# Decoder trunk on one core: the row of r by way of device memory instead of by turns on TensorE

## The chip, the cores and the metric

The kernel runs on one core of a Trainium2 chip. The metric is the device time of one execution in microseconds (us). Each kernel is run several times and the median is given.

## The reference

Two layers (DEPTH 2) of a decoder over 256 tokens (SEQ) with a width of 1024 (D). Every layer has four sub-layers, each with an RMS norm ahead of it and one behind it:

```
f = swiglu(rms_norm(h, ffn1_pre_g), ffn1_w_gu, ffn1_w_down);  h = h + 0.5 * rms_norm(f, ffn1_post_g)
u = rms_norm(h, mix_pre_g);  sb_q, sb_k, sb_v, df_q, df_k, df_v, g_sb, g_df = split(u @ w_in)
    # stick-breaking attention on sb_*, differential attention with rotary on df_*, gates, w_out
f = swiglu(rms_norm(h, ffn2_pre_g), ffn2_w_gu, ffn2_w_down);  h = h + 0.5 * rms_norm(f, ffn2_post_g)
    # then a gated per-layer embedding (w_ple_gate, w_ple_proj)

swiglu(x, w_gu, w_down) = (silu(g) * u) @ w_down,  g, u = split(x @ w_gu)        # d_ff = 2816
rms_norm(x, g) = x * r * g,  r = 1 / sqrt(mean(x * x) + eps), one number for each token
```

The inner norm's r is one number for each of the 256 tokens. It can be multiplied in behind the matrix product, since the product is linear.

## The kernel before

**Where things lie.** Tokens in natural layout: 128 tokens on the partitions, in two tiles t = 0, 1. `r_pre` is [128, 2]: the scale of token 128t + p stands on partition p, column t. A product in natural layout takes it as a scalar for each partition. In a "flat" product the outputs stand with the features on the partitions and the 256 tokens along the row. Then r is needed as a row of 256 numbers that is the same on all 128 partitions: that is `r_cols`, 256 columns of the tile `prob`.

**Who does what.** Weights come in units of 1 MB into `raw` (three slots, issued from SyncE). ScalarE (ACT) rounds a unit into `w_hi`, times the norm's gain (`high`). VectorE (DVE) writes the rest into `w_lo` (`low`). TensorE (PE) multiplies with three products for each exact one. GpSimd (POOL) computes r: `rsqrt_mean`, by `pre_norm` for the inner norms and `post_norm` for the outer ones. Its DMA queue is used at the start only, for gains and positions. Each engine has one fixed order of instructions, written out by hand; semaphores tie them together.

**An FFN** runs over 11 blocks (NC) of 256 hidden features, c = 0 to 10. Each takes three units: gate and up in two halves, then down. Block 0 and block 10 are natural; blocks 1 to 9 are flat. In a flat block VectorE's `flat_gate` adds the two halves of g (L1152), multiplies by r_cols (L1154), waits for ScalarE's silu (L726), multiplies by r_cols again (L1156), adds the two halves of u (L1158) and takes the product (L1161). Behind it stands the `low` of the second half of the next block (L1106), which TensorE needs in the middle of that block's gate and up.

**How r_cols is made before.** VectorE's `spread_r` copies r_pre over 256 columns of `mixed_t` (L1144). TensorE's `turn_r` transposes these in two turns into PSUM (L1625). ScalarE's `keep_r` copies them to r_cols (L720). This happens six times: in each layer for stage 0 (first FFN), stage 1 (mixer, for the stick-breaking q and k, used in `add_flat`, L1331) and stage 2 (second FFN). In an FFN turn_r stands in the middle of block 1, just ahead of `turn_first_ht` (L1632); in the mixer it stands behind unit m = 2.

Of the kernel before, what the change touches and what calls it, by code (L numbers as in the profile page):

```python
# [77 lines left out]
def trunk_kernel(nc, a, out):  # L78
    with ExitStack() as ctx:
# [9 lines left out]
        def bank(b):  # L89
            return ps[:, b, :]  # L90
# [2 lines left out]
            return ps[:, b:b + 2, :].rearrange("p b n -> p (b n)")  # L93


        raw = sb("raw", [P, SLOTS, UNIT])
        w_hi = sb("w_hi", [P, SLOTS, UNIT], F32R)
        w_lo = sb("w_lo", [P, SLOTS, UNIT], F32R)
# [74 lines left out]

        x_hi, x_lo = x_both[:, 0, :, :], x_both[:, 1, :, :]
        glu_g, glu_u = glu[:, 0, :, :], glu[:, 1, :, :]
        r_spread = mixed_t[:, 0:SEQ].rearrange("p (t n) -> p t n", t=TT)
        r_cols = prob[:, 0:1, 0:SEQ]
        e_ple = gates[:, 1, :, :]
        p_nat = soft[:, :, 0:PLE]
# [22 lines left out]
        g_scaled = sem("g_scaled")  # L202
        silu_scaled = sem("silu_scaled")
        h_done = sem("h_done")
        r_wide = sem("r_wide")
        r_turned = sem("r_turned")
        r_kept = sem("r_kept")
        ht_turned = sem("ht_turned")
        ht_high = sem("ht_high")
# [97 lines left out]
        HT_BANK, P_BANK, FIRST_P_BANK = 6, 7, (3, 5)  # L307
        GU_BANK = (4, 5)
        FLAT_BANK = (6, 7, 4, 5)
        FIRST_HT_BANK, R_BANK = 2, 3  # L310
        flat_g, flat_u = ([ps[:, b:b + 2, n * SEQ:(n + 1) * SEQ] for n in range(2)] for b in FLAT_BANK[::2])
        WIN_BANK = ((4, 5), (2, 3))
        DOWN_PAIR = (0, 2)
# [178 lines left out]
        def _(pool):  # L492
# [67 lines left out]
            def post_norm(i, n, order):  # L560
                for t in range(TT):
                    pool.wait_ge(squared_post, post_count(i, n, t))
                    rsqrt_mean(i, order + t, mean_post[:, t:t + 1], ms_post[:, t:t + 1], r_post[:, t:t + 1],
                               eps_half if FACTOR[n] == 0.5 else eps_norm).then_inc(post_scale, 1)

            def close(i):

                for t in range(TT):
                    pool.wait_ge(squared_post, post_count(i, 3, t))
                    rsqrt_mean(i, 18 + t, mean_post[:, t:t + 1], ms_post[:, t:t + 1], r_post[:, t:t + 1],  # L570
                               eps_norm).then_inc(post_scale, 1)
# [15 lines left out]

            for i in range(DEPTH):
                pre_norm(i, 0, 0)
                if i == 0:  # L590
                    pool.wait_ge(sines, 1)
                    pool.tensor_scalar(rope_s[:, :, 0:32], rope_s[:, :, 32:64], -1.0, None, ALU.mult
                                       ).then_inc(rope_ready, 1)
                    pool.tensor_copy(rope_c[:, :, 32:64], rope_c[:, :, 0:32]).then_inc(rope_ready, 1)
                post_norm(i, 0, 2)
                pre_norm(i, 1, 4)

                pool.wait_ge(pre_scale, 8 * i + 4)
                pool.tensor_tensor(r_query[:, :], r_pre[:, :], q_factor[:, :], ALU.mult).then_inc(query_scale, 1)
                for hd in range(DF_HEADS):  # L600
                    pool.wait_ge(d_eps, 4 * i + hd + 1)
                    pool.wait_ge(d_square, 4 * i + hd + 1)
                    rsqrt_mean(i, 6 + hd, mean_sub[:, :], ms_sub[:, :], r_sub[:, :], sub_eps
                               ).then_inc(d_scale, 1)
                post_norm(i, 1, 10)
                pre_norm(i, 2, 12)
                post_norm(i, 2, 14)
                pre_norm(i, 3, 16)
                if i < LAST:
                    close(i)  # L610
                else:
                    close_last(i)
# [3 lines left out]
        def _(act):  # L616
# [98 lines left out]
                act.wait_ge(h_done, FLAT * (2 * i + f) + c)  # L715
                act.activation(ht_hi[:, :, :], glu_u, ACT.Copy).then_inc(ht_high, 1)

            def keep_r(i, stage, b=R_BANK):
                act.wait_ge(r_turned, nth_r(i, stage))
                act.activation(r_cols[:, 0, :], bank(b)[:, 0:SEQ], ACT.Copy).then_inc(r_kept, 1)  # L720

            def flat_glu(i, f, c, u0):
                act.wait_ge(gu_done, 2 * NC * i + NC * f + c + 1)
                act.activation(glu_g, flat_g[1], ACT.Copy).then_inc(low_kept, 1)
# [21 lines left out]
            def ffn(i, f, u0, g0, next_unit, loads):  # L746

                if f:
                    first_silu(i, f, u0)
                high(i, u0 + 3, g0 + 4, halves=(0,))  # L750
                act.wait_ge(pre_scale, 8 * i + 4 * f + 2)
                silu(i, f, 0, u0 + 1, 1)
                high(i, u0 + 3, g0 + 4, halves=(1,))
                high(i, u0 + 4)
                keep_r(i, 2 * f)
                high_first_ht(i, f)
                high(i, u0 + 5, g0)
                flat_glu(i, f, 1, u0)
                high(i, u0 + 6, g0 + 4)
                with act.Fori(2, NC - 1) as c:  # L760
                    high(i, u0 + 1, c=c)
                    high_ht(i, f, c - 1)
                    high(i, u0 + 2, g0, c=c)
                    flat_glu(i, f, c, u0)
                    high(i, u0 + 3, g0 + 4, c=c)
                loads()
                high(i, u0 + 3 * NC - 2)
                high_ht(i, f, NC - 2)
                high(i, u0 + 3 * NC - 1)
                silu(i, f, NC - 1, u0 + 3 * NC - 3, 0)  # L770
                act.wait_ge(ht_split, 2 * HTS * i + HTS * f + NC - 1)
                silu(i, f, NC - 1, u0 + 3 * NC - 3, 1)
                high_last_ht(i, f, 0)
                next_unit()
                high_last_ht(i, f, 1)
# [65 lines left out]
            def mixer(i):  # L841
                for m in range(23):
# [28 lines left out]
                        diff_exp(i, DF_SCORE[m])  # L871
                    if m in DF_TURN:
                        diff_square(i, DF_TURN[m])
                    if m == 2:
                        keep_r(i, 1, QK_PAIR)
                    if m in (4, 6):
                        k = (m - 4) // 2
                        act.wait_ge(qk_turned, 2 * i + k + 1)
# [160 lines left out]
        def _(dve):  # L1039
# [98 lines left out]
                dve.tensor_tensor(ht_lo[:, :, :], src, ht_hi[:, :, :].bitcast(F32), ALU.subtract  # L1138
                                  ).then_inc(ht_split, 1)

            def spread_r(i, first=False):
                if first:
                    dve.wait_ge(const_all, 1)
                dve.tensor_copy(r_spread, r_pre[:, :].rearrange("p (t o) -> p t o", o=1).to_broadcast([P, TT, P])  # L1144
                                ).then_inc(r_wide, 1)

            def flat_gate(i, f, c):
                n = FLAT * (2 * i + f)
                wide_r = r_cols.to_broadcast([P, 2, SEQ])
# [25 lines left out]
            def ffn(i, f, u0, g0, next_unit):  # L1175
                if (i, f) not in BESIDE_INPUTS:
                    product(i, f, 0, 0)
                low(i, u0 + 3, g0 + 4, halves=(0,))
                product(i, f, 0, 1)
                spread_r(i, (i, f) == (0, 0))  # L1180
                low(i, u0 + 3, g0 + 4, halves=(1,))
                low(i, u0 + 4)
                low_ht(i, f, 0, bank(FIRST_HT_BANK).rearrange("p (k n) -> p k n", k=2))
                low(i, u0 + 5, g0)
                dve.wait_ge(r_kept, nth_r(i, 2 * f))
                flat_gate(i, f, 1)
                low(i, u0 + 6, g0 + 4)
                with dve.Fori(2, NC - 1) as c:
                    low(i, u0 + 1, c=c)
                    low_ht(i, f, c - 1, glu_u)  # L1190
                    low(i, u0 + 2, g0, c=c)
                    flat_gate(i, f, c)
                    low(i, u0 + 3, g0 + 4, c=c)
                if (i, f) == (0, 0):
                    fold_cosine()
                low(i, u0 + 3 * NC - 2)
                low_ht(i, f, NC - 2, glu_u)
                low(i, u0 + 3 * NC - 1)
                for t in range(TT):
                    product(i, f, NC - 1, t)  # L1200
                low_last_ht(i, f, 0)
                next_unit()
                low_last_ht(i, f, 1)
# [117 lines left out]
            def add_flat(i, j, x):  # L1321

                n = 4 * i + 2 * (j - SBQ) + x + 1
                dst = (sbq_t, sbk_t)[j - SBQ][:, 2 * x:2 * x + 2, :]
                dve.wait_ge(flat_kept, n)
                dve.scalar_tensor_tensor(out=dst, in0=flat_pair(SB_FLAT[j][x])[0],
                                         scalar=SB_D ** -0.5 if j == SBQ else 1.0, in1=flat_copy,
                                         op0=ALU.mult, op1=ALU.add).then_inc(flat_added, 1)
                dve.wait_ge(flat_added, n)
                dve.wait_ge(r_kept, nth_r(i, 1))  # L1330
                dve.tensor_tensor(dst, dst, r_cols.to_broadcast([P, 2, SEQ]), ALU.mult).then_inc(sb_ready, 1)  # L1331

            def mixer(i):
                if i == 0:
                    dve.wait_ge(rope_ready, 2)
                dve.wait_ge(pre_scale, 8 * i + 4)
                spread_r(i)
                dve.wait_ge(query_scale, i + 1)
                for m in range(23):

# [200 lines left out]
        def _(pe):  # L1541
# [77 lines left out]
                        elif s == 1 and done is not None:  # L1619
                            mm.then_inc(done, 1)  # L1620

            def turn_r(i, stage, b):
                pe.wait_ge(r_wide, nth_r(i, stage))
                for t in range(TT):
                    mm = pe.transpose(bank(b)[:, t * P:(t + 1) * P], r_spread[:, t, :], ident[:, :])  # L1625
                mm.then_inc(r_turned, 1)

            def turn_first_ht(i, f):
                turn_r(i, 2 * f, R_BANK)
                for k in range(2):  # L1630
                    for t in range(TT):
                        mm = pe.transpose(bank(FIRST_HT_BANK)[:, k * SEQ + t * P:k * SEQ + (t + 1) * P],  # L1632
# [23 lines left out]
            def ffn(i, f, q, u0, before_last):  # L1656
# [58 lines left out]
                def step(c, at, first=False):  # L1715
# [6 lines left out]
                    if first:  # L1722
                        turn_first_ht(i, f)
                    flat_gate_up(u0, 1, c, at)
                    if first:
                        pe.wait_ge(r_kept, nth_r(i, 2 * f))
                    down(u0 + 1, c - 1, first=first, c=at)

                def first_gate_up(s, t, before):
# [134 lines left out]

            def behind(i, m):

                if m == 2:
                    turn_r(i, 1, QK_PAIR)
                if m == 4:
                    pe.wait_ge(r_kept, nth_r(i, 1))  # L1870
                    pe.wait_ge(roped, 4 * i + 2)
                    turn_four(pair(QK_PAIR), df_slabs[0]).then_inc(qk_turned, 1)
                if m == 6:
# [241 lines left out]
```

## Time and profile before

| | |
|---|---|
| median of 3 runs | 1174.3 us (1174.22 to 1174.74) |
| the profiled execution | 1173.8 us; its span from the first to the last instruction 1172.1 us |
| granted TensorE clock, mean over the span | 0.999 of full speed |
| TensorE busy | 1163.3 us, 99% of the span |
| VectorE, ScalarE, GpSimd busy | 850.1, 720.6 and 51.6 us (73%, 61%, 4%) |
| DMA from memory | 213.68 MB read, 183 GB/s over the span |

The times in the trace are microseconds from the first instruction. A line such as L1625 is the line of the kernel that issues the instruction. PEld is TensorE's load of the stationary tile, which overlaps the multiplication before it. So the distance from one load's start to the next is what an instruction costs TensorE in a dense stretch. A row of the timeline merges equal instructions: start, time in all, engine, line, operation, tiles, shape, count.

### The profile page before, as it was taken

To read this page: it belongs to the slowest core of one execution; us is meant where nothing else is said; L and a number is where in the kernel's file an instruction comes from. 1 tells how busy PE (TensorE), PEld (TensorE's weight loads), DVE (VectorE), ACT (ScalarE), POOL (GpSimd) and SP (SyncE) were. 2 spreads that over 40 slices of the span, in tenths; PEclk is the share of its full clock that TensorE was granted. 3 is DMA by queue.
4 is the path that set the end of the run, shared out by engine and by line. 5 is a ranking of instruction groups with operands and counts; after the bars stand their busy time and mean duration, and the time that the engine had idled before them with its cause. 6 is when DMAs were issued, how large, how long until landed. Compare 5 with 4: busy or idle time off the path is not lost.

```text
span 1172.1 us, 17196 instructions
## 1 busy us (share of the span) xinstructions
PE 1163.3 (99%) x6031; PEld 983.4 (84%) x6031; DVE 850.1 (73%) x1290; ACT 720.6 (61%) x1166; POOL 51.6 (4%) x124
## 2 busy tenths in 40 slices
PE   9999999999999999999999999999999999999997
PEld 7888888888888888888888888888888888888886
DVE  6766777977857776676787776678776677677666
ACT  7555556677765655555685655565776566565555
POOL 4000001000000000000100000010000010000002
PEclk9999999999999999999999999999999999999999
DMA  9656565654354555655556565756534456656551
GB/s 296 217 189 205 176 216 164 220 179 145 128 196 144 194 201 189 205 176 210 180 173 200 173 207 180 243 172 192 169 109 179 164 162 214 194 172 207 182 194 37
DMA packets 138655, 215.37 MB, mean 184 GB/s; under 512 B 6958, under 2 KB 97904, under 8 KB 138608
## 3 DMA queue, kind: packets, MB, share of 16 engines
q1 hardware_dynamic: 135808, 208.43, 53.4%
q10 hardware_dynamic: 2576, 6.29, 1.6%
q8 instruction: 28, 0.46, 0.2%
q14 instruction: 19, 0.16, 0.0%
q0 software_dynamic: 224, 0.04, 0.0%
HBM read 213.68 MB, written 1.05 MB: 183 GB/s over the span
## 4 chain that ended last, share of the span: by engine, by line
PE 99%; DVE 0%; issue 0%; POOL 0%; ACT 0%; POOLq 0%; DVEq 0%
PE ps L1671 23%; PE ps L1544 19%; PE ps L1546 18%; PE ps L1545 18%; PE ps L1681 12%; PE ps L1914 3%; PE ps L1591 2%; PE ps L1923 1%; PE ps L1800 1%; PE ps L1815 1%; PE ps L1774 0%; PE ps L1786 0%; PE ps L2006 0%; PE ps L1829 0%; PE ps L1836 0%
## 5 line engine op out<-in xcount | busy, mean ns | idle before, releaser
L1106 DVE SCALAR_TENSOR_TENSOR w_lo<-raw,g_layer,w_hi 128x512 fp32r<-128x512 f32 (+1 forms) x504 | 356.3, 767 | 139.1 <-ACT w_hi L644 139.1
L644 ACT ACTIVATE w_hi<-raw,g_layer 128x512 fp32r<-128x512 f32 (+1 forms) x524 | 346.7, 732 | 113.7 <-PE ps L1681 97.0
L1671 PE MATMUL ps<-x_both,w_hi 128*128 128x512 f32 x1152 | 287.7, 392 | 0.0
L1671 PEld LDWEIGHTS ps<-x_both,w_hi 128*128 128x128 f32 x1152 | 209.3, 189 | 39.4 <-issue 0.4
L1544 PE MATMUL ps<-w_hi,x_both 128*128 128x512 f32 x576 | 231.6, 402 | 0.0
L1546 PE MATMUL ps<-w_hi,x_both 128*128 128x512 f32 x576 | 224.9, 390 | 0.0
L1545 PE MATMUL ps<-w_lo,x_both 128*128 128x512 f32 x576 | 224.5, 390 | 0.0
L1103 DVE TENSOR_TENSOR w_lo<-raw,w_hi 128x1024 fp32r<-128x1024 f32 x114 | 134.8, 1220 | 61.3 <-ACT w_hi L641 61.3
L641 ACT ACTIVATE w_hi<-raw 128x1024 fp32r<-128x1024 f32 x114 | 114.7, 1052 | 92.7 <-PE ps L1546 92.6
L1681 PEld LDWEIGHTS ps<-x_both,w_lo 128*128 128x128 f32 x1152 | 152.6, 191 | 8.4
L1681 PE MATMUL ps<-x_both,w_lo 128*128 128x256 f32 x1152 | 156.0, 283 | 0.0
L1544 PEld LDWEIGHTS ps<-w_hi,x_both 128*128 128x128 f32 x576 | 108.2, 188 | 25.8 <-issue 3.0
L1546 PEld LDWEIGHTS ps<-w_hi,x_both 128*128 128x128 f32 x576 | 108.1, 188 | 23.3
L1545 PEld LDWEIGHTS ps<-w_lo,x_both 128*128 128x128 f32 x576 | 108.4, 188 | 19.9
L1544 PE MATMUL ps<-w_hi,ht_hi 128*128 128x512 f32 x320 | 124.9, 390 | 0.0
L1546 PE MATMUL ps<-w_hi,ht_lo 128*128 128x512 f32 x320 | 124.6, 389 | 0.0
L1545 PE MATMUL ps<-w_lo,ht_hi 128*128 128x512 f32 x320 | 124.5, 389 | 0.0
L726 ACT ACTIVATE glu<-glu 128x512 f32<-128x512 f32 x36 | 22.8, 633 | 78.5 <-DVE glu L1154 78.5
L1546 PEld LDWEIGHTS ps<-w_hi,ht_lo 128*128 128x128 f32 x320 | 60.1, 188 | 12.5
L1545 PEld LDWEIGHTS ps<-w_lo,ht_hi 128*128 128x128 f32 x320 | 60.1, 188 | 12.3
L1544 PEld LDWEIGHTS ps<-w_hi,ht_hi 128*128 128x128 f32 x320 | 60.1, 188 | 12.3
L1156 DVE TENSOR_TENSOR glu<-glu,prob 128x512 f32<-128x512 f32 x36 | 24.9, 693 | 27.6 <-ACT glu L726 27.6
(230 smaller groups left out, 1039.1 us busy)
## 6 DMA issues: line engine op xcount, KB each, us to landing
raw<-in_ffn_w_gu SPq DMA_DIRECT2D x170, 512.0 KB, 4.6
raw<-in_ffn_w_down SPq DMA_DIRECT2D x88, 512.0 KB, 4.0
raw<-in_w_in SPq DMA_DIRECT2D x80, 512.0 KB, 4.5
raw<-in_w_out SPq DMA_DIRECT2D x16, 512.0 KB, 4.0
raw<-in_w_ple_gate SPq DMA_DIRECT2D x16, 512.0 KB, 3.7
raw<-in_w_branch_sb SPq DMA_DIRECT2D x8, 512.0 KB, 4.1
raw<-in_w_branch_diff SPq DMA_DIRECT2D x8, 512.0 KB, 4.0
raw<-in_ffn_w_gu SPq DMA_DIRECT2D x12, 256.0 KB, 7.4
```

The source lines that it names most:

```text
L641: last = act.activation(w_hi[:, s, part], raw[:, s, part], ACT.Copy)
L644: last = act.activation(w_hi[:, s, part], raw[:, s, part], ACT.Copy, scale=g_layer[:, g:g + 1])
L1103: last = dve.tensor_tensor(w_lo[:, s, part], raw[:, s, part], whi[:, part], ALU.subtract)
L1106: last = dve.scalar_tensor_tensor(out=w_lo[:, s, part], in0=raw[:, s, part], scalar=g_layer[:, g:g + 1], in1=whi[:, part], op0=ALU.mult, o ...
L1156: dve.tensor_tensor(glu_g, glu_g, wide_r, ALU.mult).then_inc(silu_scaled, 1)
L1544: pe.matmul(dst, x_h, w_h, start=first, stop=False, **group)
L1545: pe.matmul(dst, x_h, w_l, start=False, stop=False, **group)
L1546: return pe.matmul(dst, x_l, w_h, start=False, stop=last, **group)
L1591: mm = pe.transpose(x_bank(i, q, idx)[:, k * P:(k + 1) * P], src[:, (4 * n + k) * P:(4 * n + k + 1) * P], ident[:, :])
L1671: mm = pe.matmul(dst, w_hi[:, s, cols], x_both[:, :, 4 * half + k, :], start=half == 0 and k == 0, stop=stop and k == 3, skip_group_check= ...
L1681: mm = pe.matmul(bank(FLAT_BANK[j])[:, 0:SEQ], w_lo[:, s, cols], x_hi[:, 4 * half + k, :], start=False, stop=False, skip_group_check=True)
L1914: mm = pe.matmul(dst, w_hi[:, s, cols], x_both[:, :, 4 * half + k, :], start=half == 0 and k == 0, stop=stop and k == 3, skip_group_check= ...
```

## The change

GpSimd makes the row by three DMAs and no other engine has a part in it. For each stage, behind both r's, it writes r_pre[:, 0] and r_pre[:, 1] (128 numbers of 4 bytes each, one for each partition) to a row of a buffer in device memory, waits until both are there, and reads the row of 256 numbers (1 KB) back to all 128 partitions of r_cols. spread_r, turn_r and keep_r go, and so do TensorE's two waits for r_kept. VectorE's waits for r_kept stay where they were and count by 16.

```
+            def keep_row(i, stage):
+
+                n = nth_r(i, stage)
+                for t in range(TT):
+                    pool.wait_ge(pre_scale, 8 * i + 2 * stage + t + 1)
+                    pool.dma_start(r_rows[n - 1, t * P:(t + 1) * P].rearrange("(p o) -> p o", o=1), r_pre[:, t:t + 1]
+                                   ).then_inc(r_written, 16)
+                pool.wait_ge(r_written, 32 * n)
+                pool.dma_start(r_cols[:, 0, :], r_rows[n - 1, :].partition_broadcast(P)).then_inc(r_kept, 16)
...
             for i in range(DEPTH):
                 pre_norm(i, 0, 0)
+                keep_row(i, 0)
...
                 pool.tensor_tensor(r_query[:, :], r_pre[:, :], q_factor[:, :], ALU.mult).then_inc(query_scale, 1)
+                keep_row(i, 1)
...
                 pre_norm(i, 2, 12)
+                keep_row(i, 2)
                 post_norm(i, 2, 14)
...
-            def keep_r(i, stage, b=R_BANK):
-                act.wait_ge(r_turned, nth_r(i, stage))
-                act.activation(r_cols[:, 0, :], bank(b)[:, 0:SEQ], ACT.Copy).then_inc(r_kept, 1)
...
-            def spread_r(i, first=False):
-                if first:
-                    dve.wait_ge(const_all, 1)
-                dve.tensor_copy(r_spread, r_pre[:, :].rearrange("p (t o) -> p t o", o=1).to_broadcast([P, TT, P])
-                                ).then_inc(r_wide, 1)
...
-                dve.wait_ge(r_kept, nth_r(i, 2 * f))
+                dve.wait_ge(r_kept, 16 * nth_r(i, 2 * f))
                 flat_gate(i, f, 1)
...
-                dve.wait_ge(r_kept, nth_r(i, 1))
+                dve.wait_ge(r_kept, 16 * nth_r(i, 1))
                 dve.tensor_tensor(dst, dst, r_cols.to_broadcast([P, 2, SEQ]), ALU.mult).then_inc(sb_ready, 1)
...
-            def turn_r(i, stage, b):
-                pe.wait_ge(r_wide, nth_r(i, stage))
-                for t in range(TT):
-                    mm = pe.transpose(bank(b)[:, t * P:(t + 1) * P], r_spread[:, t, :], ident[:, :])
-                mm.then_inc(r_turned, 1)
-
             def turn_first_ht(i, f):
-                turn_r(i, 2 * f, R_BANK)
...
                     flat_gate_up(u0, 1, c, at)
-                    if first:
-                        pe.wait_ge(r_kept, nth_r(i, 2 * f))
                     down(u0 + 1, c - 1, first=first, c=at)
...
-                if m == 2:
-                    turn_r(i, 1, QK_PAIR)
                 if m == 4:
-                    pe.wait_ge(r_kept, nth_r(i, 1))
                     pe.wait_ge(roped, 4 * i + 2)
```

## Rows read from the trace of the kernel before

**Rows 1.** The page: span and busy time of each engine.

```profile
span 1172.1 us, 17196 instructions
PE 1163.3 (99%) x6031; PEld 983.4 (84%) x6031; DVE 850.1 (73%) x1290; ACT 720.6 (61%) x1166; POOL 51.6 (4%) x124
```

**Rows 2.** Who PEld waited for: us in total, times, longest.

```profile
PEld ps L1544 <- DVE x_both L1133: 2.5, 10, 0.3
PEld ps L1591 <- DVE h L1222: 1.8, 9, 0.2
```

**Rows 3.** PEld timeline about turn_r: first FFN and mixer of layer 1.

```profile
610.02 0.24 PEld L1625 LDWEIGHTS ps<-ident,mixed_t 128*128 128x128 f32 x2
610.24 0.47 PEld L1632 LDWEIGHTS ps<-ident,glu 128*128 128x128 f32 x4
...
794.83 0.19 PEld L1546 LDWEIGHTS ps<-w_hi,x_both 128*128 128x128 f32 x1
795.06 0.37 PEld L1625 LDWEIGHTS ps<-ident,mixed_t 128*128 128x128 f32 x2
795.40 0.19 PEld L1544 LDWEIGHTS ps<-w_hi,x_both 128*128 128x128 f32 x1
795.51 0.19 PEld L1545 LDWEIGHTS ps<-w_lo,x_both 128*128 128x128 f32 x1
```

**Rows 4.** The tiles prob and mixed_t: durations ns min/median/max, first and last start.

```profile
L720 ACT ACTIVATE prob<-ps x6: 383/384/384, 31.1 to 974.8; 128x256 f32<-128x256 f32 x6
L1144 DVE COPY mixed_t<-r_pre x6: 280/281/317, 27.6 to 970.5; 128x256 f32<-128x256 f32 x6
```

**Rows 5.** POOL timeline: the last r of stages 0, 1 and 2 (layer 0), 0 (layer 1).

```profile
25.00 0.55 POOL L552 TENSOR_TENSOR r_pre<-ms_pre,neg_half 128x1 f32<-128x1 f32 x1
208.38 0.19 POOL L599 TENSOR_TENSOR r_query<-r_pre,q_factor 128x2 f32<-128x2 f32 x1
386.71 0.55 POOL L552 TENSOR_TENSOR r_pre<-ms_pre,neg_half 128x1 f32<-128x1 f32 x1
604.44 0.55 POOL L552 TENSOR_TENSOR r_pre<-ms_pre,neg_half 128x1 f32<-128x1 f32 x1
```

**Rows 6.** DVE timeline: first use of r_cols and what follows, by the same stages.

```profile
36.77 0.69 DVE L1154 TENSOR_TENSOR glu<-glu,prob 128x512 f32<-128x512 f32 x1
...
40.54 2.73 DVE L1106 SCALAR_TENSOR_TENSOR w_lo<-raw,g_layer,w_hi 128x512 fp32r<-128x512 f32 x4
232.53 0.69 DVE L1331 TENSOR_TENSOR sbq_t<-sbq_t,prob 128x512 f32<-128x512 f32 x1
401.05 0.69 DVE L1154 TENSOR_TENSOR glu<-glu,prob 128x512 f32<-128x512 f32 x1
404.51 2.73 DVE L1106 SCALAR_TENSOR_TENSOR w_lo<-raw,g_layer,w_hi 128x512 fp32r<-128x512 f32 x4
616.20 0.69 DVE L1154 TENSOR_TENSOR glu<-glu,prob 128x512 f32<-128x512 f32 x1
```

**Rows 7.** PE timeline: block 2 of the first FFN of layer 0.

```profile
46.98 2.08 PE L1681 MATMUL ps<-x_both,w_lo 128*128 128x256 f32 x16
```

**Rows 8.** pos_i's issues; the landings of pos_i, lam_layer, post_g, out_h, in this order.

```profile
L504 POOL DMA_DIRECT2D pos_i<-in_positions x2: 547/572/597, 4.5 to 5.1; - x2
DMA to landing us min/median/max: 5.6/5.6/5.6
...
DMA to landing us min/median/max: 4.5/5.4/6.3
...
DMA to landing us min/median/max: 3.3/5.1/7.1
...
DMA to landing us min/median/max: 2.0/2.0/2.1
```

**Rows 9.** One of POOL's and one of DVE's rows at the end of the second FFN.

```profile
568.85 1.26 POOL L550 TENSOR_TENSOR ms_pre<-mean_pre,eps_norm 128x1 f32<-128x1 f32 x1 [3.42 <-ACT tmp L682]
568.78 2.47 DVE L1106 SCALAR_TENSOR_TENSOR w_lo<-raw,g_layer,w_hi 128x1024 fp32r<-128x1024 f32 x2
```

More of the change, by code:

```diff
@@ L93, in pair @@
             return ps[:, b:b + 2, :].rearrange("p b n -> p (b n)")
+        r_rows = nc.dram_tensor("r_rows", (3 * DEPTH, SEQ), F32, kind="Internal").ap()
         raw = sb("raw", [P, SLOTS, UNIT])
@@ L175, in trunk_kernel @@
         glu_g, glu_u = glu[:, 0, :, :], glu[:, 1, :, :]
-        r_spread = mixed_t[:, 0:SEQ].rearrange("p (t n) -> p t n", t=TT)
         r_cols = prob[:, 0:1, 0:SEQ]
@@ L204, in trunk_kernel @@
         h_done = sem("h_done")
-        r_wide = sem("r_wide")
-        r_turned = sem("r_turned")
+        r_written = sem("r_written")
         r_kept = sem("r_kept")
@@ L309, in trunk_kernel @@
         FLAT_BANK = (6, 7, 4, 5)
-        FIRST_HT_BANK, R_BANK = 2, 3
+        FIRST_HT_BANK = 2
         flat_g, flat_u = ([ps[:, b:b + 2, n * SEQ:(n + 1) * SEQ] for n in range(2)] for b in FLAT_BANK[::2])
@@ L754, in ffn @@
                 high(i, u0 + 4)
-                keep_r(i, 2 * f)
                 high_first_ht(i, f)
@@ L873, in mixer @@
                         diff_square(i, DF_TURN[m])
-                    if m == 2:
-                        keep_r(i, 1, QK_PAIR)
                     if m in (4, 6):
@@ L1179, in ffn @@
                 product(i, f, 0, 1)
-                spread_r(i, (i, f) == (0, 0))
                 low(i, u0 + 3, g0 + 4, halves=(1,))
@@ L1336, in mixer @@
                 dve.wait_ge(pre_scale, 8 * i + 4)
-                spread_r(i)
                 dve.wait_ge(query_scale, i + 1)
@@ L1865, in behind @@
             def behind(i, m):
-                if m == 2:
-                    turn_r(i, 1, QK_PAIR)
                 if m == 4:
-                    pe.wait_ge(r_kept, nth_r(i, 1))
                     pe.wait_ge(roped, 4 * i + 2)
```

## The prediction

> **What bounds the kernel now.** I read the page first: TensorE is busy in 1163.3 us of a span of 1172.1, at a granted clock of 0.999 of full speed, and no other engine is above 73% [rows 1]. Then the waits: among what stopped TensorE's loads I looked for VectorE, ScalarE or a DMA that is late in the middle of a stage. There is none. What VectorE makes it wait for is 2.5 and 1.8 us over 19 places, the turned inputs and the updated h between stages [rows 2]. None of them stands in the stretches where the row of r is made. So the reader is to see a TensorE that works through its own list. A change is worth what it takes off that list, unless it makes something late by more than the lead that the others have. Two questions follow: what do twelve turns cost in a dense stretch, and how late may the row come?
>
> **What goes from TensorE.** The cost of a turn is not its duration in the trace but how far it pushes the next load. In an FFN the two loads of turn_r start at 610.02 and the next group starts at 610.24: 0.22 us for both [rows 3]. In the mixer they start at 795.06 and the next product's load at 795.40, which looks like 0.34; but that next load is followed at 0.11 by another, where the usual distance of these rows is 0.23 (794.83 to 795.06), so 0.12 of it is caught up at once, and 0.22 stays [rows 3]. Six pairs at 0.22 us make 1.3 us. If nothing were caught up in the two mixers it would be 4 x 0.22 + 2 x 0.34 = 1.6 us. I take 1.3.
>
> **What goes from the others.** ScalarE loses six copies of 0.38 us and the waits ahead of them, VectorE six copies of 0.28 us [rows 4]. Both engines are ahead of TensorE there, for none of its loads waits for them in these stretches [rows 2]; I cost this at nothing. If that lead were not there, the gain would be at most 6 x (0.38 + 0.28) = 4.0 us. TensorE's two kinds of waits for r_kept go too. They held nothing up: it had no wait in the stretch.
>
> **What comes.** On GpSimd, for each of six stages: two writes of 128 numbers, a wait, and a read of 128 KB in all. What is queued behind the wait on GpSimd is, in stages 0 and 2, the outer norm at the far end of the FFN; in stage 1 r_query is already issued ahead of it, and the differential attention's scales come only behind the first use of the row (232.53 [rows 6]). So nobody waits for GpSimd itself. The added traffic is 6 x 128 KB, 0.8 MB beside 214 MB; nothing.
>
> The row's way, counted from the end of the last r: GpSimd issues two DMAs of 0.57 us one behind the other, so the second starts 0.6 us on. It is of the shape of the positions at the start (128 x 4 bytes, same engine, the other direction), which landed 5.6 us after its issue [rows 8]. Then the read. The nearest row is diff_lambda, 128 KB spread from 1 KB to all partitions, though from another queue: 5.4 us [rows 8]. That makes 0.1 + 0.6 + 5.6 + 5.4 = 11.7 us. The lower bound takes the fastest landing of the trace, 2.0 us for the stores at the quiet end [rows 8], twice: 4.7 us. The upper bound adds to each of the three issues what GpSimd's small operations lost beside a long VectorE one (1.26 us in rows 9, where a small tensor operation takes 0.19 in rows 5: a loss of 1.07 us [rows 5, 9]), and takes 7.1 for the read instead of 5.4 (the slowest broadcast of post_g [rows 8]): 11.7 + 3.2 + 1.7 = 16.6 us. I take 11.7, because its two terms are the rows of the same shapes.
>
> **When it is needed.** First use minus end of the last r: stage 0 of layer 0, 36.77 - 25.55 = 11.2 us; stage 0 of layer 1, 616.20 - 604.99 = 11.2; the second FFN, 401.05 - 387.26 = 13.8 in layer 0 and the same in layer 1; the mixer, 232.53 - 208.57 = 24.0 [rows 5, 6]. So by 11.7 the mixers and second FFNs never see it, and in the two first FFNs VectorE stands still for about 0.5 us, plus the 0.2 us by which TensorE is now earlier: 0.7 us each.
>
> **What is late next.** Behind that wait come the silu, the product and the low of block 2's second half, which ends at 40.54 + 2.73 = 43.27. TensorE needs it halfway through the sixteen products that start at 46.98 (eight belong to the first half, at about 0.12 us each), at 47.9 [rows 6, 7]. The lead is 4.7 us. In the other FFNs the low ends 3.46 + 2.73 us behind L1154 as in the second FFN (404.51 - 401.05 [rows 6]) and not 3.77 + 2.73, so their lead is 5.0. Less the 0.2: the row may take 15.7 us in the first FFN of layer 0, 16.0 in that of layer 1, 18.6 in the second ones before TensorE loses anything. A wait of 0.7 us costs nothing.
>
> The sum: the profiled execution took 1173.8 us, its span and 1.7 around it. 1173.8 - 1.3 = 1172.5; the median of the runs stands 0.5 above that execution, so 1174.3 - 1.3 = **1173.0 us**. At the upper bound of the way (16.6 us) TensorE would lose 0.9 + 0.6 = 1.5 us: 1174.5. At the lower nothing changes in the sum.
>
> **A page's rule on this way.** The Trainium skill, "DMA: Bandwidth & Descriptors", section "Anatomy of one DMA — SWDGE (gpsimd) path", gives about 2.0 us fixed for each such DMA; the way would be an estimated 4.7 us or so and no engine would see it, where the rows at the start show 5.6 us for one. By either the time is the same, 1173.0.
>
> **The rivals.**
>
> (a) *GpSimd's issues are held up by VectorE (slower).* VectorE works in most of the stretch between the last r and the first use of the row, and one operation of GpSimd was stretched by about 1 us when a long one of VectorE ran beside it [rows 9]. If each of the three issues had to sit out a whole group of four L1106 (2.73 us [rows 6]), the way would be 11.7 + 8.2 = 19.9 us. TensorE would lose 4.2, 3.9, 1.3 and 1.3 us in the four FFNs, 10.7 in all: 1174.3 - 1.3 + 10.7 = 1183.7 us. The way decides from where the losses of the first FFNs pass 1.3 + 2.3 us, at 17.7 us. Against it: the operations of r in the same stretches took 0.55 us undisturbed [rows 5], and the loss in rows 9 is 1 us and not 2.7. The positions' issues took 0.55 to 0.60 us [rows 8], but at a time when VectorE had hardly begun, so they don't bear on it. The Trainium skill, "SBUF — State Buffer", section "SBUF: two separate sides", says that GpSimd can't write descriptors while VectorE is in a mode that takes both ports, and tells of 620 ns that became 3100; the operations here are of kinds with two inputs, which by its section "Who interferes with whom" contend with GpSimd's reads only. No row here shows an issue beside a busy VectorE. 7 in 100.
>
> (b) *The relief of ScalarE and VectorE counts (faster).* If their 0.66 us per stage were on the way to TensorE in all six stages, the time would be 1173.0 - 4.0 = 1169.0; if it only took off the waits between stages (2.5 + 1.8 us, half of them), 1170.9. For it: ScalarE's copy could only start behind TensorE's turns, so it stood still there. Against it: the waits of rows 2 stand at the stage's start, ahead of the turns, and none behind them. 7 in 100.
>
> (c) *The change does nothing that can be seen.* The turns may lie in holes: a saving of 0 to 1.3 us, 1173.0 to 1174.3, together with small losses by late rows up to 1174.9. It gives "same" like my forecast. 20 in 100.
>
> The forecast, 1172.2 to 1173.6, has 66 in 100.
>
> **How the numbers follow.** A measurement of this kernel tells some 0.2% (2.3 us) from no change: 1171.95 to 1176.65. (b) and the tail of the forecast make faster 0.08; (a) makes slower 0.07; the rest, 0.85, is same. The range takes the forecast and (c) and the bound of the late row: 1171.9 to 1174.9, which leaves out (a) and most of (b), 14 in 100.
>
> **What would show it.** Right: L1625, L720 and L1144 are gone, and the four loads of L1632 follow the product before them at 0.2. The read's landing is at 9 to 13 us behind the last r; L1154 of block 1 in the first FFNs starts 0 to 1.5 us later with a DMA as its releaser, and TensorE shows no wait in block 2. The span is 1170.8. Wrong: waits of PEld for w_lo (L1106) or for VectorE's L1158 in block 2 of an FFN, which would be (a); or fewer waits between stages, (b). GpSimd's issues in the middle of the kernel, by their duration beside 0.57, decide between (a) and the rest.

## The result, and the profile after

The kernel before took 1174.21 us (median of 20 runs, 1174.03 to 1174.91), the changed one 1176.37 us (20 runs, 1175.35 to 1178.33): a ratio of 1.0018, 95% interval 1.0012 to 1.0024. The forecast was 1173.0 us, range 1171.9 to 1174.9. So the change costs 2.2 us where 1.3 were to be gained. It lies inside the 0.2% that I called "same", but outside the range, and its interval is clear of no change. The runs also spread over 3 us where those of before spread over 1.

The page after: span, busy times, and the chain that ended last, by engine; the last line is that chain in the page before.

```profile
span 1175.3 us, 17174 instructions
PE 1163.4 (99%) x6019; PEld 982.3 (84%) x6019; DVE 848.1 (72%) x1284; ACT 718.2 (61%) x1160; POOL 62.1 (5%) x142
PE 94%; DMA 3%; DVE 1%; ACT 1%; issue 0%; POOL 0%; DVEq 0%; POOLq 0%; ACTq 0%
...
PE 99%; DVE 0%; issue 0%; POOL 0%; ACT 0%; POOLq 0%; DVEq 0%
```

TensorE has its twelve turns less (6019 against 6031 in [rows 1]), and the chain now holds 3% of DMA, where before it held none and was TensorE's at 99%. Who TensorE's loads waited for, to be read against [rows 2]:

```profile
PEld ps L1662 <- DVE glu L1152: 3.2, 2, 1.7
...
PEld ps L1542 <- DVE x_both L1139: 2.5, 10, 0.4
...
PEld ps L1589 <- DVE h L1221: 2.0, 10, 0.2
...
PEld ps L1672 <- DVE w_lo L1112: 1.1, 2, 0.6
```

Two lines are new, the first and the last: the add of g's halves (L1152), and the low of block 2 (L1112 now). Together they are 4.3 us, two times each. The add frees the bank of g, the part of PSUM that TensorE's next products for g go to. The way of the row that leads to them, in the first FFN of layer 0: GpSimd's, VectorE's and TensorE's timeline.

```profile
25.34 0.56 POOL L552 TENSOR_TENSOR r_pre<-ms_pre,neg_half 128x1 f32<-128x1 f32 x1
25.85 1.20 POOL L571 DMA_DIRECT2D r_rows<-r_pre  x2
36.68 0.55 POOL L574 DMA_DIRECT2D prob<-r_rows  x1 [9.63 <-DMA r_rows<-r_pre]
...
43.16 0.69 DVE L1152 TENSOR_TENSOR glu<-ps,glu 128x512 f32<-128x512 f32 x1 [6.90 <-DMA prob<-r_rows]
...
43.91 1.69 PEld L1662 LDWEIGHTS ps<-x_both,w_hi 128*128 128x128 f32 x8 [1.68 <-DVE glu L1152]
...
50.13 1.02 PEld L1672 LDWEIGHTS ps<-x_both,w_lo 128*128 128x128 f32 x8 [0.57 <-DVE w_lo L1112]
```

The last r ends at 25.90. The second write is issued at about 26.5; the chain gives it 9.9 us, and GpSimd issues the read at 36.7. The read takes 6.5 more. VectorE stands still for 6.9 us, and TensorE for 1.68 and 0.57 us. In layer 1 the same:

```profile
606.74 1.12 POOL L571 DMA_DIRECT2D r_rows<-r_pre  x2
617.18 0.54 POOL L574 DMA_DIRECT2D prob<-r_rows  x1 [9.33 <-DMA r_rows<-r_pre]
...
623.88 0.69 DVE L1152 TENSOR_TENSOR glu<-ps,glu 128x512 f32<-128x512 f32 x1 [3.63 <-DMA prob<-r_rows]
...
624.63 1.68 PEld L1662 LDWEIGHTS ps<-x_both,w_hi 128*128 128x128 f32 x8 [1.52 <-DVE glu L1152]
...
630.85 1.01 PEld L1672 LDWEIGHTS ps<-x_both,w_lo 128*128 128x128 f32 x8 [0.57 <-DVE w_lo L1112]
```

Losses of 2.25 and 2.09 us, less the 1.3 us of the turns, are +3.0 us. The span of this execution is 3.2 us above that of before (1175.3 against 1172.1); it took 1177.09 us, 0.7 above the median. The issues themselves, by the tile r_rows (ns, min/median/max), and the median us to landing, from the DMA view:

```profile
L571 POOL DMA_DIRECT2D r_rows<-r_pre x12: 537/561/662, 25.9 to 970.6; - x12
...
prob<-r_rows POOLq DMA_DIRECT2D x6, 128.0 KB, 6.6
...
r_rows<-r_pre POOLq DMA_DIRECT2D x12, 0.5 KB, 8.3
```

The issues are as short as those of the positions in [rows 8] (0.54 to 0.66 us against 0.55 to 0.60): what is long comes behind the issue.

### The profile page after: what moved, and what is told of

It reads as the page before. It is cut to its first block, busy times and chain, and to the rows that moved or that the text cites. A ratio compares the mean times of both kernels' runs of the same rounds, so it can differ in the third digit from the quotient of the medians.

```text
span 1175.3 us, 17174 instructions
## 1 busy us (share of the span) xinstructions
PE 1163.4 (99%) x6019; PEld 982.3 (84%) x6019; DVE 848.1 (72%) x1284; ACT 718.2 (61%) x1160; POOL 62.1 (5%) x142
## 4 chain that ended last, share of the span: by engine, by line
PE 94%; DMA 3%; DVE 1%; ACT 1%; issue 0%; POOL 0%; DVEq 0%; POOLq 0%; ACTq 0%
PE ps L1662 21%; PE ps L1542 18%; PE ps L1544 18%; PE ps L1543 18%; PE ps L1672 11%; PE ps L1900 2%; DMA r_rows<-r_pre 2%; PE ps L1589 1%; PE ps L1909 1%; DMA prob<-r_rows 1%; PE ps L1789 1%; PE ps L1804 1%; PE ps L1763 0%; PE ps L1775 0%; DVE w_lo L1112 0%
## 5 line engine op out<-in xcount | busy, mean ns | idle before, releaser
L1112 DVE SCALAR_TENSOR_TENSOR w_lo<-raw,g_layer,w_hi 128x512 fp32r<-128x512 f32 (+1 forms) x504 | 356.3, 767 | 131.2 <-ACT w_hi L657 131.1
```

The source lines that it names most:

```text
L1112: last = dve.scalar_tensor_tensor(out=w_lo[:, s, part], in0=raw[:, s, part], scalar=g_layer[:, g:g + 1], in1=whi[:, part], op0=ALU.mult, o ...
```

## The experiments

**The row without the writes (given_row).** Does lateness alone cost, and is 1.3 us there to be had? The row then holds 256 numbers of a gain instead of r, so the outputs are wrong; only the time counts.

```
-                for t in range(TT):
-                    pool.wait_ge(pre_scale, 8 * i + 2 * stage + t + 1)
-                    pool.dma_start(r_rows[n - 1, t * P:(t + 1) * P].rearrange("(p o) -> p o", o=1), r_pre[:, t:t + 1]
-                                   ).then_inc(r_written, 16)
-                pool.wait_ge(r_written, 32 * n)
-                pool.dma_start(r_cols[:, 0, :], r_rows[n - 1, :].partition_broadcast(P)).then_inc(r_kept, 16)
+                pool.wait_ge(pre_scale, 8 * i + 2 * stage + 2)
+                pool.dma_start(r_cols[:, 0, :], a["ffn1_pre_g"][i, 0:SEQ].partition_broadcast(P)).then_inc(r_kept, 16)
```

> The changed kernel without the two writes and without the wait for them: r_cols is read from 256 numbers of an input (a norm's gain) as soon as both r's are there, so the row's contents are not r and the outputs differ. Theory A (lateness alone costs): the row lands about 7 us behind the last r, before its first use at 10.5; no engine waits; 1174.2 - 1.3 = 1172.9 us. Rival B (the added DMAs or the relieved engines cost or bring something themselves): another time than that, 1174.2 or more if the traffic costs, below 1172 if the relief of ScalarE and VectorE counts.

Measured: 1173.08 us (11 runs) beside 1174.37 for the kernel before; ratio 0.9989 (0.9980 to 0.9998). That is 1.3 us less, as the sum had it; the interval allows 0.2 to 2.3. Its profile has no new wait of TensorE in any FFN. So the added read, GpSimd's part and the relief of the other two engines leave nothing that this measurement can see. The writes are not in this run, so it says nothing of what they do to others.

**Each pair of turns twice (turns_twice)**, in the kernel before.

```
-                for t in range(TT):
+                for t in (0, 1, 0, 1):
                     mm = pe.transpose(bank(b)[:, t * P:(t + 1) * P], r_spread[:, t, :], ident[:, :])
```

> The kernel before with each pair of turns of r made twice (12 more turns, same result). If a pair costs TensorE 0.22 us: 1174.2 + 1.3 = 1175.5 us. If turns lie in holes: 1174.2. If they cost their modelled duration (0.27 us each): 1174.2 + 3.3 = 1177.5.

Measured: 1175.82 us (11 runs), ratio 1.0012 (1.0003 to 1.0021): 1.45 us for six pairs, 0.24 us a pair. The distance of loads in [rows 3] gave 0.22. Turns in holes (1174.2) and turns at the duration that the profile shows (1177.5) both lie outside.

**Single DMAs, each waited for by GpSimd alone (probes)**, in the kernel before, behind the r's of stage 0; two more from ScalarE's queue.

```
+            def probe(dst, src):
+                n_probe[0] += 1
+                pool.dma_start(dst, src).then_inc(probed, 16)
+                pool.wait_ge(probed, 16 * n_probe[0])
...
+                    act.dma_start(hbm_hw4[2 * i + n, :].rearrange("(p o) -> p o", o=1), r_pre[:, 0:1]
+                                  ).then_inc(probed_hw, 16)
```

> The kernel before with single DMAs on GpSimd's queue behind the r's of stage 0, each waited for by GpSimd alone: 128 x 4 bytes to device memory, 128 x 512 bytes to device memory, 128 x 4 bytes from it, 1 KB from it to all partitions, 128 x 4 bytes within SBUF to one partition, one row of 512 bytes to device memory; and on ScalarE's queue two writes of 128 x 4 bytes at the end of the FFN. Theory W (small pieces written to device memory are slow to be confirmed): the 4-byte writes land in about 8 us, also from ScalarE's queue, the 4-byte reads in about 5.6, the 512-byte writes and the one within SBUF in 2 to 5. Theory Q (GpSimd's queue is slow beside the weights' traffic, whatever the shape): all GpSimd's landings 6 to 9 us, ScalarE's 2 to 5. Theory V (two writes one behind the other slow each other): a single 4-byte write 5.6 us, as the read at the start. The time itself should stay at 1174.2 us, since no engine waits for these.

The time was 1174.55 us in one run. The DMA view, with the queue, the count, KB each and the median us to landing (the names' trailing digits are left out by the profile):

```profile
hbm_w<-r_pre POOLq DMA_DIRECT2D x6, 0.5 KB, 9.7
hbm_hw<-r_pre ACTq DMA_DIRECT2D x4, 0.5 KB, 8.9
hbm_w<-ident POOLq DMA_DIRECT2D x6, 64.0 KB, 6.4
got_r<-hbm_w POOLq DMA_DIRECT2D x6, 0.5 KB, 4.4
got_wide<-in_ffn_pre_g POOLq DMA_DIRECT2D x6, 128.0 KB, 4.9
line<-r_pre POOLq DMA_DIRECT2D x3, 0.5 KB, 5.2
hbm_line<-ident POOLq DMA_DIRECT2D x3, 0.5 KB, 3.9
lam_layer<-in_diff_lambda ACTq DMA_DIRECT2D x2, 128.0 KB, 11.8
```

The same 128 x 4 bytes take 4.4 us when read, 5.2 within SBUF and 9.7 when written to device memory; a write of 512 bytes in one piece takes 3.9. ScalarE's queue is no better (8.9), so it isn't a matter of GpSimd's queue: theory Q falls. A single write is as slow as a pair: theory V falls. Theory W stands. Note the last row: diff_lambda's load, which stands behind the two added writes (and two loads of gains) on ScalarE's queue, landed in 11.8 us where it had taken 5.4 [rows 8].

**What about the small pieces is slow (probes_shape)**, again single DMAs in the kernel before.

```
+                    probe(w_dense[k, :].rearrange("(p o) -> p o", o=1), r_pre[:, 0:1])
+                    probe(w_apart[k, :, 0:1], r_pre[:, 0:1], allow_slow_non_contiguous=True)
+                    probe(w_far[k, :, 0:1], r_pre[:, 0:1], allow_slow_non_contiguous=True)
+                    probe(w_sixteen[k, :, :], ident[:, 0:16])
+                    probe(one_line[0:1, :], r_pre[:, 0:1])
+                    probe(spread_line[:, :], one_line[0:1, :].rearrange("o (a n) -> o a n", a=1).to_broadcast([1, P, P]))
```

> The kernel before with single DMAs on GpSimd's queue behind the r's of stage 0, each waited for by GpSimd alone. To device memory: 128 numbers side by side (w_dense), 128 numbers 64 bytes apart (w_apart), 128 numbers 512 bytes apart (w_far), 128 pieces of 64 bytes (w_sixteen). Within SBUF: 128 numbers to one partition (one_line), and from there 512 bytes to all partitions (spread_line). Theory W1 (small pieces in one stretch of memory hinder each other): w_dense 9 to 10 us, w_apart or w_far 4 to 6. Theory W2 (any 4-byte write to device memory is slow to be confirmed): all three 9 to 10, w_sixteen 5 to 7. Theory W3 (any write of 128 small packets is slow, the 64-byte pieces too): all four 9 to 10. Within SBUF 4 to 6 us each by all three. The time stays 1174.3 us.

```profile
w_dense<-r_pre POOLq DMA_DIRECT2D x6, 0.5 KB, 8.3
w_apart<-r_pre POOLq DMA_DIRECT2D x6, 0.5 KB, 6.3
w_far<-r_pre POOLq DMA_DIRECT2D x6, 0.5 KB, 4.4
w_sixteen<-ident POOLq DMA_DIRECT2D x6, 8.0 KB, 3.6
one_line<-r_pre POOLq DMA_DIRECT2D x6, 0.5 KB, 3.4
spread_line<-one_line POOLq DMA_DIRECT2D x6, 64.0 KB, 4.0
```

128 numbers side by side took 8.3 us (7.1 to 9.2 in six writes), 64 bytes apart 6.3 (5.3 to 7.1), 512 bytes apart 4.4 (2.3 to 4.8); 64-byte pieces side by side 3.6 (1.7 to 5.1). So neither 4 bytes nor 128 pieces are slow by themselves. They are slow when many of them go to one short stretch of device memory: W1 of the three. The stretch isn't all of it: pieces of 64 bytes side by side and numbers 64 bytes apart cover the same 8 KB in the same steps, and the small ones took 2.7 us longer. The order of the six DMAs was always the same, and no run turned it. Which part of the memory's path does it isn't shown.

**VectorE's wait behind the add of g (behind_add, behind_add_again).**

```
                 dve.tensor_tensor(glu_g, flat_g[0], glu_g, ALU.add).then_inc(prod_done, 1)
                 dve.wait_ge(prod_done, prod + 1)
+                if first:
+                    dve.wait_ge(r_kept, 16 * nth_r(i, 2 * f))
                 dve.tensor_tensor(glu_g, glu_g, wide_r, ALU.mult).then_inc(g_scaled, 1)
...
-                dve.wait_ge(r_kept, 16 * nth_r(i, 2 * f))
-                flat_gate(i, f, 1)
+                flat_gate(i, f, 1, True)
```

> The changed kernel with VectorE's wait for the row moved behind the add of g's halves in block 1 (ahead of the first multiplication by the row). Theory A (the row lands 17 to 18 us behind the last r, and the wait, which stands ahead of the add, keeps the bank of g from TensorE as well as w_lo): TensorE's waits of 1.7 and 1.5 us for the add in block 2 go, the waits for w_lo grow to about 1.6 and 1.1 us because VectorE's list is only 0.7 us shorter; in all 1.5 us less than the changed kernel, about 1174.9 us. Rival B (the loss is not at the wait: traffic of the added DMAs, GpSimd's work beside VectorE): 1176.4 us, as the changed kernel.

Measured: 1177.4 us (7 runs, 1175.8 to 1181.2), ratio 1.0028 (1.0016 to 1.0039); not the 1174.9 that I expected. In its profile the waits for L1152 are gone, but the row was later than in the changed kernel's (a write landed after up to 11.0 us, against 9.9), and the stall had moved to the bank of u, 0.8 and 3.8 us, with 0.6 for the low. What the changed kernel would have taken there wasn't known, since the writes' landing differs from one measurement to the next. So both ran again side by side on one chip.

> The changed kernel as it is, beside the others of this call on one chip. Theory A (the time follows how late the row lands in the two first FFNs): about 1176.4 us again, with more spread than the kernel before has.

> The changed kernel with VectorE's wait behind the add of g's halves, once more, now beside the changed kernel on the same chip. In the trace of the first of these the stall had moved to the bank of u (3.8 us in layer 1) and TensorE's granted clock fell behind it. [...] Rival: the place matters as I first worked out, 1.5 us less in every run.

Measured: the changed kernel 1180.46 us (5 runs, 1179.8 to 1182.4), ratio 1.0056 (1.0042 to 1.0069); with the wait behind the add 1177.7 (9 runs), ratio 1.0026 (1.0016 to 1.0036). That is 2.8 us less than the changed kernel beside it, more than the 1.5 us of the rival. Not all of it is shown to be the place of the wait. In the first FFN of layer 0 TensorE lost 1.2 + 0.6 us at a way of 17.7 us, so a way of 15.9 costs nothing with the wait behind the add, where 15.0 is the limit ahead of it (worked out further down): 0.9 us for each late FFN. But in these two profiles the row of layer 0's second FFN was also there after 17.7 us instead of 19.2, and with it no stall. How the 2.8 us divide isn't shown. The expectation that the changed kernel would show 1176.4 again was wrong: it took 4 us more than in its first measurement. Its trace says where from: the row was late in three FFNs instead of two.

```profile
44.03 1.68 PEld L1662 LDWEIGHTS ps<-x_both,w_hi 128*128 128x128 f32 x8 [1.91 <-DVE glu L1152]
...
409.38 1.68 PEld L1662 LDWEIGHTS ps<-x_both,w_hi 128*128 128x128 f32 x8 [1.05 <-DVE glu L1152]
415.61 1.01 PEld L1672 LDWEIGHTS ps<-x_both,w_lo 128*128 128x128 f32 x8 [0.57 <-DVE w_lo L1112]
...
627.40 1.70 PEld L1662 LDWEIGHTS ps<-x_both,w_hi 128*128 128x128 f32 x8 [2.53 <-DVE glu L1152]
633.62 1.01 PEld L1672 LDWEIGHTS ps<-x_both,w_lo 128*128 128x128 f32 x8 [0.56 <-DVE w_lo L1112]
```

With 0.57 more for the low in the first FFN of layer 0 the stalls are 7.2 us; less 1.3 that is 5.9, and the span is 1178.1, 6.0 above that of before.

**Stage 0 by turns, stages 1 and 2 by memory (stage0_turned).** The row of stage 0 is made as in the kernel before; keep_row(i, 1) and keep_row(i, 2) stay.

```
                 pre_norm(i, 0, 0)
-                keep_row(i, 0)
...
+                if f == 0:
+                    keep_r(i, 0)
...
+                if f == 0:
+                    spread_r(i, i == 0)
...
+                if f == 0:
+                    turn_r(i, 0, R_BANK)
```

> The row of stage 0 is made by turns of TensorE as before, those of stages 1 and 2 by GpSimd by way of device memory. Theory A: four pairs of turns are saved and no FFN stalls, since the second FFNs allow 18 us and the mixer 24: 1174.3 - 0.9 = 1173.4 us. Rival B (the added DMAs or GpSimd's waits cost in every stage): 1174.3 or more.

Measured: 1175.16 us (11 runs, 1173.7 to 1176.6), ratio 1.0007 (0.9998 to 1.0016), not 1173.4. In this measurement the row of the second FFNs was late too: VectorE began the add at 406.00 in layer 0, 18.8 us behind the last r, and TensorE's waits for L1152 and the low were 1.0 and 1.2 us in all over both layers. Less 0.9 for four pairs that is +1.3; its span is 1173.4, also +1.3. Rival B, a cost in every stage, isn't needed.

**The row by way of SBUF (within_sbuf).**

```
-        r_rows = nc.dram_tensor("r_rows", (3 * DEPTH, SEQ), F32, kind="Internal").ap()
+        r_line = sb("r_line", [1, SEQ])
...
-                    pool.dma_start(r_rows[n - 1, t * P:(t + 1) * P].rearrange("(p o) -> p o", o=1), r_pre[:, t:t + 1]
+                    pool.dma_start(r_line[0:1, t * P:(t + 1) * P], r_pre[:, t:t + 1]
...
-                pool.dma_start(r_cols[:, 0, :], r_rows[n - 1, :].partition_broadcast(P)).then_inc(r_kept, 16)
+                pool.dma_start(r_cols[:, 0, :], r_line[0:1, :].rearrange("o (a n) -> o a n", a=1).to_broadcast([1, P, SEQ])).then_inc(r_kept, 16)
```

> The changed kernel with the row put together in one partition of SBUF instead of in device memory: two DMAs of 128 x 4 bytes from r_pre to a line of 1 KB, and one DMA from that line to all partitions. Theory W (the confirmation of 4-byte pieces written to device memory is what is slow): the writes land in 2 to 6 us and the row is there 8 to 13 us behind the last r, within what the others allow; no stall of TensorE, 1174.3 - 1.3 = 1173.0 us. Rival Q (any DMA of GpSimd's with 4-byte pieces is slow here): 9 us and 17 in all, 1176.4.

Measured: 1172.97 us (11 runs, 1172.6 to 1173.7), ratio 0.9989 (0.9980 to 0.9998), and once more:

> The row by way of one partition of SBUF, once more, to see whether the gain of 1.3 us over the kernel before stands: 1173.0 us. If it was the chip or the round: 1174.3.

1172.87 us (11 runs, 1172.6 to 1173.2), ratio 0.9988 (0.9979 to 0.9997). In its profile, GpSimd's and VectorE's timeline in the first FFN of layer 1:

```profile
604.89 1.12 POOL L571 DMA_DIRECT2D r_line<-r_pre  x2
610.81 0.54 POOL L574 DMA_DIRECT2D prob<-r_line  x1 [4.80 <-DMA r_line<-r_pre]
...
617.50 0.69 DVE L1152 TENSOR_TENSOR glu<-ps,glu 128x512 f32<-128x512 f32 x1 [2.19 <-DMA prob<-r_line]
```

The row is there 12.6 us behind the last r (617.50 - 604.94). VectorE still waits, 3.8 us in two FFNs, and TensorE for none of it. This version beats the kernel before by what the forecast had promised.

## Why the prediction was wrong, point by point

**What goes from TensorE: right.** 0.22 us a pair, 1.3 in all. Turns made twice cost 1.45 us, given_row gained 1.3, within_sbuf 1.35. Rival (c), turns in holes, falls.

**What goes from the others: right. The traffic: right for the time, but not "nothing".** given_row has ScalarE and VectorE relieved and the added read, and comes within 0.1 us of 1173.0; rival (b) falls. What I left out is what the writes do to the weights' loads. In the changed kernel the gate and up units issued near the row's way took 6.3 to 9.3 us to land in the four FFNs, where the kernel before had 4.4 to 4.7 and given_row 4.5 to 4.8. ScalarE and VectorE stood still for it (3.0 and 3.7 us in the first FFN of layer 1). The row came later still, so the time doesn't show it.

**The row's way: this step failed.** I took 11.7 us from the last r, as the sum of 5.6 for the write and 5.4 for the read. Measured were 17.3 and 17.1 us in the two first FFNs, 16.1 and 17.2 in the second ones (405.44 and 987.30 against the ends of the last r); in after_again up to 19.2. The larger part is the write, 9.9 and 9.6 us in the two first FFNs instead of 5.6. I priced it by the positions' load, of the same shape but in the other direction. 128 numbers written side by side to device memory land in 8.3 to 9.7 us, read from there in 4.4; written 512 bytes apart they land in 4.4 too. So it isn't the direction alone, but writing them side by side. The read was 6.6 instead of 5.4. With the two measured ways in place of 11.7 and nothing else changed, the prediction's own sum loses 1.6 + 1.1 us and gives 1175.7: outside the range by this step alone. My upper bound of 16.6 was put together from the wrong mechanism, a held-up issue, and was still too low. The fastest landing of the trace as a lower bound was of large stores and told nothing of small ones either.

**When it is needed: misread by one instruction.** I counted to the first multiplication by the row (L1154). But the wait stands at the head of flat_gate, ahead of the add L1152, as the diff shows. So the row is needed 0.7 us earlier. In the kernel before the add started here, with no wait, and the multiplication 0.7 us behind it:

```profile
615.49 0.68 DVE L1152 TENSOR_TENSOR glu<-ps,glu 128x512 f32<-128x512 f32 x1
```

The add needs no r, and it frees the bank of g that block 2 begins with. That bank is what TensorE waited for first. I named the low as what is late next and not this bank.

**How long it may take: right but for that, within 0.3 us.** I said 15.7, 16.0 and 18.6 us. Less the 0.7 it is 15.0, 15.3 and 17.9. Measured, way less loss: 17.26 - 2.25 = 15.0 and 17.09 - 2.09 = 15.0 in the first FFNs; in the second one of after_again 19.2 - 1.6 = 17.6.

**The outcome.** My rival (a) had the right consequence and its price in the right form, but the wrong mechanism: GpSimd's issues took 0.54 to 0.66 us also where VectorE was busy beside them (1.0 of the 1.2 us of the issues at 606.7), and ScalarE's queue was no faster with the same write (8.9 us). So no issue was held up. The rule of the Trainium skill, "SBUF — State Buffer", section "SBUF: two separate sides", found no case here; by its section "Who interferes with whom" it should not have, and the trace agrees. The fixed 2.0 us for a DMA of the Trainium skill, "DMA: Bandwidth & Descriptors", section "Anatomy of one DMA — SWDGE (gpsimd) path", was undercut by single landings (1.7 us for 64-byte pieces, 1.9 within SBUF); the median of the dense 4-byte write was four times as much, and there the measurement decides. A sentence of the same section, that the delay comes from the confirmation and can be surprisingly long "especially when the write target is HBM", fits this write (9.7 us, against 5.2 within SBUF), but not every small one: 512 bytes apart the same numbers landed in device memory in 4.4 us. I hadn't weighed it.

**The chance.** Slower by over 0.2% had 7 in 100. The first measurement gave 0.18%, the later one 0.56%. The range's upper end was built on the belief that the shape was priced.

## What to carry to other kernels

Price a DMA by a row of the same direction and the same pieces, not by one of the same size: many 4-byte pieces written side by side to device memory are the slow case here, and a row gathered within SBUF is not. When work goes off the bound engine and comes back as a chain of DMAs, find the wait in the code, not the first use of the data, and ask what stands between the two. A lead is all or nothing: in the first FFNs a way below 15 us costs nothing, above it every microsecond costs one, and its scatter becomes the kernel's.

## What the runs showed of the hardware that I hadn't expected

**A stall can cost the clock too.** In the profile of behind_add TensorE stood still for 3.8 us in one piece. Behind it its granted clock was 0.50, the level of 1.2 GHz instead of 2.4. TensorE's loads, and the windows with busy times of PE, PEld, DVE, ACT and POOL, then the granted clock, the DMA share and GB/s:

```profile
629.82 3.06 PEld L1663 LDWEIGHTS ps<-x_both,w_hi 128*128 128x128 f32 x8 [3.76 <-DVE glu L1160]
...
636.00 1.69 PEld L1663 LDWEIGHTS ps<-x_both,w_hi 128*128 128x128 f32 x8
...
625.00:630.00 5.00, 1.44 (x11) 1.20 (x10) 2.11 (x4) 2.18 (x4) 0.00 (x0) 0.84 0.72 255
630.00:635.00 5.00, 5.00 (x16) 4.23 (x17) 5.00 (x7) 3.80 (x6) 0.00 (x0) 0.50 0.07 16
635.00:640.00 5.00, 5.00 (x31) 4.49 (x31) 4.37 (x7) 3.16 (x5) 0.00 (x0) 0.98 1.01 353
```

The same 24 loads that took from 411.12 to 414.88 in the changed kernel's profile took from 629.82 to 636.00 here: 2.4 us more for a stall of 3.8. The length of the stall alone doesn't tell. In behind_add_again one of 2.0 us was followed by the low clock as well (the first two lines), and 24 loads took 5.3 us instead of 3.8. In after_again the longest, 2.5 us, was not (the last line, the same window).

```profile
628.14 2.73 PEld L1663 LDWEIGHTS ps<-x_both,w_hi 128*128 128x128 f32 x8 [1.98 <-DVE glu L1160]
628.00:631.00 3.00, 2.85 (x8) 2.23 (x9) 2.90 (x6) 3.00 (x5) 0.00 (x0) 0.60 0.07 25
...
628.00:631.00 3.00, 3.00 (x18) 2.61 (x17) 2.14 (x5) 2.83 (x5) 0.00 (x0) 1.00 0.51 171
```

**Small writes get in each other's way, and in the way of loads on other queues.** They landed in 8.3 us side by side and in 4.4 at a distance of 512 bytes. The weights come by SyncE's queue, and they landed later beside such writes too. These are ScalarE's wait for them and their landings among the issues from 604 to 622 us, first FFN of layer 1, in the changed kernel; the last two lines are the same landings in the kernel before:

```profile
616.14 2.57 ACT L657 ACTIVATE w_hi<-raw,g_layer 128x512 fp32r<-128x512 f32 x4 [3.01 <-DMA raw<-in_ffn_w_gu]
raw<-in_ffn_w_gu SPq DMA_DIRECT2D x6, 512.0 KB, 8.8
raw<-in_ffn_w_down SPq DMA_DIRECT2D x2, 512.0 KB, 12.6
...
raw<-in_ffn_w_gu SPq DMA_DIRECT2D x6, 512.0 KB, 4.4
raw<-in_ffn_w_down SPq DMA_DIRECT2D x2, 512.0 KB, 4.9
```

From 612 to 617 us the core moved 34 GB/s, where the kernel before moved 348 from 610 to 615. Behind the two writes on ScalarE's queue in probes it was 18 GB/s from 174 to 180 us, against 264 in the kernel before. In within_sbuf the gate and up loads took 5.1 and 5.0 us in the first FFNs, where the changed kernel had 9.3 and 8.8; in the second ones they took 6.6 and 7.1, no less than there (6.3 and 7.3). No TensorE wait came from it in any of these runs, so what it would cost a kernel with a shorter lead on its weights isn't shown.

**The landing differs from one measurement to the next.** For the changed kernel that means medians of 1176.4 and 1180.5 us, where the kernel before stayed within 0.2 us in all measurements. What makes it differ isn't shown.
